# A two-block transformer kernel: 64 instead of 32 gathered tokens, 57 of 128 up tiles multiplied unsplit, and the second block's modulation read later

## The reference, cut to what matters

```python
q = (h2 @ w_query).reshape(T, 8, 2, 128)              # 256 tokens
sc = einsum('thpc,hpnc->thpn', q, sub_keys)           # scores against 2 x 128 keys
s1, i1 = top_k(sc[..., 0, :], 16); s2, i2 = top_k(sc[..., 1, :], 16)
cand = s1[..., :, None] + s2[..., None, :]            # 16 x 16 candidates per head
top_s, sel = top_k(cand, 16); idx = i1 * 128 + i2 of the selected
gates = softmax(top_s)
a = gelu(einsum('cd,chkd->chk', h2, expert_u[idx])) * gates
out = einsum('chk,chkd->cd', a, expert_v[idx])
x = x + gt2 * out
```

## Time and profile before

| | |
|---|---|
| median of three runs | 2063.39 us |
| profiled execution, its span | 2061.18 us, 2059.4 us |
| TensorE busy | 1984.0 us (96% of the span), 14228 matmul instructions |
| VectorE busy | 1667.9 us (81%) |
| ScalarE busy | 1270.3 us (62%) |
| GpSimd busy | 426.7 us (21%) |
| mean granted TensorE clock | 0.988 |
| moved by DMA | 476.51 MB, 231 GB/s in the mean |
| the chain that ended last | PE 75%, DVE 11%, ACT 5%, DMA 4%, issue 4%, POOL 2% |

### The profile page before, as it was taken

One profiled execution on the slowest core, in us unless ns is written; L12 is line 12 of the kernel. 1 busy time (PEld: TensorE's weight loads), 2 busy tenths in 40 slices (PEclk: granted clock), 3 DMA queues, 4 the chain that ended last, 5 costly groups with the idle time before them and its releaser, 6 DMA issues.

```text
span 2059.4 us, 37734 instructions
## 1 busy us (share of the span) xinstructions
PE 1984.0 (96%) x14228; PEld 1883.2 (91%) x14228; DVE 1667.9 (81%) x3456; ACT 1270.3 (62%) x2369; POOL 426.7 (21%) x384
## 2 busy tenths in 40 slices
PE   7999999999999999999989998999999999999997
PEld 5998999999999998999889898999999999999997
DVE  3777669898888888999779655699998898888886
ACT  3355556666999655555455454566669996555554
POOL 0000002425100133444100000034340001443340
PEclk9999999999999999999999999999999999999999
DMA  8765566666544699999766533666665446999994
GB/s 350 267 225 164 178 200 210 210 213 194 176 127 132 214 346 365 365 363 374 262 226 247 204 113 102 200 209 212 209 197 171 134 127 208 329 326 324 322 320 141
DMA packets 125156, 476.51 MB, mean 231 GB/s; under 512 B 13808, under 2 KB 14320, under 8 KB 120112
## 3 DMA queue, kind: packets, MB, share of 16 engines
q1 hardware_dynamic: 99168, 362.86, 52.8%
q0 software_dynamic: 20704, 80.55, 10.4%
q10 hardware_dynamic: 5104, 30.69, 3.9%
HBM read 472.14 MB, written 1.05 MB: 230 GB/s over the span
## 4 chain that ended last, share of the span: by engine, by line
PE 75%; DVE 11%; ACT 5%; DMA 4%; issue 4%; POOL 2%; ACTq 0%; DVEq 0%
PE PB L964 16%; PE PB L936 9%; PE PB L551 8%; PE PB L553 8%; PE PB L552 8%; PE PB L965 8%; PE PB L934 5%; PE PB L910 5%; DVE WL L1713 3%; DMA RING<-in_v 3%; ACT WH L1241 2%; PE PB L860 2%; POOL AR L2484 2%; PE PB L933 1%; DVE AR L1738 1%
## 5 line engine op out<-in xcount | busy, mean ns | idle before, releaser
L1713 DVE TENSOR_TENSOR WL<-RING,WH 128x1024 fp32r<-128x1024 f32 x651 | 801.7, 1232 | 262.1 <-ACT WH L1241 259.4
L1241 ACT ACTIVATE WH<-RING 128x1024 fp32r<-128x1024 f32 x651 | 686.8, 1056 | 390.3 <-PE PB L965 200.0
L964 PE MATMUL PB<-HX,WH 128*128 128x448 f32 x2048 | 646.8, 376 | 7.7 <-DVE WL L1713 6.5
L965 PE MATMUL PB<-HX,WL 128*128 128x224 f32 x2048 | 538.8, 263 | 0.0
L964 PEld LDWEIGHTS PB<-HX,WH 128*128 128x128 f32 x2048 | 383.7, 187 | 41.4 <-issue 11.0
L551 PE MATMUL PB<-HX,WH 128*128 128x224 f32 (+1 forms) x1360 | 394.7, 290 | 10.5 <-DVE HX L1792 5.7
L965 PEld LDWEIGHTS PB<-HX,WL 128*128 128x128 f32 x2048 | 390.2, 191 | 0.0
L552 PE MATMUL PB<-HX,WH 128*128 128x224 f32 (+1 forms) x1360 | 381.1, 280 | 0.0
L553 PE MATMUL PB<-HX,WL 128*128 128x224 f32 (+1 forms) x1360 | 381.0, 280 | 0.0
L936 PE MATMUL PB<-HX,WH 128*128 128x448 f32 x1162 | 375.6, 375 | 0.0
L934 PE MATMUL PB<-HX,WL 128*128 128x224 f32 x1328 | 326.3, 266 | 0.0
(11 more groups left out here) (265 smaller groups left out, 2712.7 us busy)
## 6 DMA issues: line engine op xcount, KB each, us to landing
RING<-in_u SPq DMA_DIRECT2D x256, 512.0 KB
RING<-in_v SPq DMA_DIRECT2D x256, 512.0 KB
RING<-in_win SPq DMA_DIRECT2D x90, 512.0 KB
AR<-in_wr ACTq DMA_DIRECT2D x24, 1024.0 KB, 7.9
RING<-in_wq SPq DMA_DIRECT2D x32, 512.0 KB
AR<-in_wr POOLq DMA_DIRECT2D x12, 1024.0 KB, 5.6
AR<-in_wm SPq DMA_DIRECT2D x8, 1024.0 KB, 16.3
RING<-in_wout SPq DMA_DIRECT2D x16, 512.0 KB
```

Source lines behind the costliest of these rows:

```text
L964: e.matmul(both_parts(c), hi(n_v + n)[:, cs], dense(k), start=start, stop=False)
L965: return e.matmul(PB[c][:, 0:T], lo(n_v + n)[:, cs], HH[:, k, 0:T], start=False, stop=stop)
L1241: e.activation(hi(t), raw(("w", t), words(t)), ACT.Copy).then_inc(s_hi, 1)
L1713: e.tensor_tensor(lo(t), raw(("w", t), words(t)), hi(t).bitcast(F32), ALU.subtract).then_inc(s_lo, 1)
```

## The change

`SP` becomes 64: 192 tokens are dense, 64 sparse; GK becomes 64, so 64 dots and 64 sums of gathered rows per block, and NQ becomes 48. Half 1 of the choice comes first, so the sparse tokens' experts are known after the first half of the choice. Then the indices are packed, brought to `SPX`, and the first three gathers issued, between the two halves on GpSimd. The dots stand beside the gates, at up tiles j = 83 to 127 (one or two in each); the 64 sums stay in the down stage, from tile 4 on. Up tiles with j >= 83 or j % 7 == 5 (45 and 12, together 57 in each block) are not split: TensorE waits for the tile in `RING` and multiplies it as fp32 with the unsplit activations `HT`. A ring slot that held such a tile is free when TensorE has used it. The modulation's chunks: 8 in the first block's down stage (from tile 12 on), 8 in the second mixer as before, and the last 8 beside the second mixer's gates, all eight in one buffer (`ar(0, 2, D)`), each issued when the one before is summed; `bcast(1, ...)` moves behind them, ahead of the output projection. Areas in `AR` move, `HT` and the choice's among them.

```diff
-SP = 32
+SP = 64
...
-SPARSE = {}
-for _m in range(N_GATHER):
-    SPARSE.setdefault(2 + _m * 119 // N_GATHER, []).append(_m)
-GELU_AT = 3 + GK * 119 // N_GATHER
+EARLY = 0
+DOT_AT = {}
+for _m in range(GK):
+    DOT_AT.setdefault(46 + 2 * _m if _m < EARLY else JG - 1 + (_m - EARLY) * (NK - JG + 1) // (GK - EARLY), []).append(_m)
+SUM_AT = {}
+for _m in range(GK, N_GATHER):
+    SUM_AT.setdefault(4 + (_m - GK) * 119 // GK, []).append(_m)
+GELU_AT = 2
+RAW = [j >= JG - 1 or j % 7 == 5 for j in range(NK)]
+RAW_TILE = [any(RAW[j] and n == w + j for w in (W_U, W2_U) for j in range(NK)) for n in range(N_TILES)]
...
-V_FIRST = 22
-N_IN_V = 12
+V_FIRST = 12
+N_IN_V = 8
+N_MID = 8
...
-WIDE = [j < JG - 1 for j in range(NK)]
+WIDE = [not RAW[j] for j in range(NK)]
...
# sync_program
-                    if was == "w":
-                        e.wait_ge(s_lo, n + 1)
+                    if was == "w" and RAW_TILE[n]:
+                        e.wait_ge(s_used, n + 1)
+                    elif was == "w":
+                        e.wait_ge(s_lo, SPLIT[n])
...
# tensor_program, peer
-                                r = three(PB[b][:, 0:T], wh[:, m, :], wl[:, m, :], HH[:, m, 0:T], HL[:, m, 0:T],
-                                          m == 0, m == KT - 1)
+                                r = e.matmul(PB[b][:, 0:T], w[:, m, :], HT[:, m, 0:T], start=m == 0, stop=m == KT - 1)
...
# tensor_program, second mixer: out of the Q tiles, to the output projection
-                if c == 0:
-                    bcast(1, (6, 7))
...
+            bcast(1, (0, 6))
...
# vector_program, choose: after the first half
+                    if o == 0:
+                        ts = slice(128 - SP, 128)
+                        own.done(own.n)
+                        e.wait_ge(s_gi, 2 * blk + 1)
+                        e.wait_ge(s_key, 4 * blk + 4)
...
# vector_program, peer: up tiles, after gates and times
+                    for m in DOT_AT.get(j, ()):
+                        gathered(m)
...
# vector_program, second mixer: late_sums() out at four of its 12 calls, one added after each pair of gate tiles
+                late_sums()
...
+            e.wait_ge(s_mdv, 24)
+            add_rows(48 + 2 * N_IN_V, 96, C_B2 + 2 * N_IN_V, 1)
+            e.wait_ge(s_mod, 10)
+            bcast(1, MC[:, 64:72])
...
# gpsimd_program, peer: between the halves, and at the end
+                    if o == 0:
+                        e.wait_ge(s_pk, blk + 1)
+                        for g in range(128 // SP):
+                            e.dma_start(SPX[SP * g:SP * g + SP, :, :], PK[128 - SP:128, g, :, :]).then_inc(s_sx, 16)
+                        e.wait_ge(s_sx, 16 * (128 // SP) * (blk + 1))
+                        gathers(N_BUF)
+                gathers(N_GATHER)
...
# gpsimd_program, between the blocks
+                if g < 24 + N_IN_V + N_MID:
+                    e.wait_ge(s_mdv, max(N_IN_V, g - 25))
+                else:
+                    e.wait_ge(s_mdv, g - 24)
+                    e.wait_ge(s_ps, 4)
```

More of the change, by code:

```diff
@@ L104 @@
 CHOICE = [80, 55] * 16 + [110, 150] + [105] * 8 + [55, 120] + [125, 125, 60, 125, 150, 125, 90] + [125, 125, 60, 125, 150, 125]
-CHOSEN = {len(CHOICE) * a + 43: a for a in range(2)}
+CHOSEN = {len(CHOICE) * o + 43: o for o in range(2)}
 def choice_turns():
@@ L1999, in choose @@
             def choose(blk):
-                for a in range(2):
+                for o in range(2):
+                    a = 1 - o
                     f2 = [0, 0]
@@ L2447, in peer, with gathers, beside @@
                     e.dma_start(HROW[SP * g:SP * g + SP, :], HROW[0:SP, :]).then_inc(s_hd, 16)
-                def add_halves(j0, j1):
+                issued = 0
+                def gathers(n):
+                    nonlocal issued
+                    for m in range(issued, n):
+                        M = N_GATHER * blk + m
+                        if M >= N_BUF:
+                            e.wait_ge(s_spent, M - N_BUF + 1)
+                        e.indirect_dma_start(
+                            out=GB[:, M % N_BUF, :], out_offset=None, in_=ur if m < GK else v,
+                            in_offset=bass.IndirectOffsetOnAxis(ap=SPX[:, 0, m % GK:m % GK + 1].bitcast(U32), axis=0),
+                        ).then_inc(s_gb[M % N_BUF], 16)
+                    issued = max(issued, n)
+                def beside(o, j0, j1):
                     for j in range(j0, j1):
@@ L2453, in add_halves @@
                             e.tensor_tensor(PG[:, j, :], PG[:, j, :], PG[:, j + 1, :], ALU.add).then_inc(s_sump, 1)
-                for a in range(2):
+                        if o:
+                            gathers(N_BUF + sum(len(DOT_AT.get(i, ())) for i in range(j + 1)))
+                for o in range(2):
+                    a = 1 - o
                     vv = V16[:, a, :, :].rearrange("p (h s) k -> p h s k", s=2)
                     ff = IF[:, a, :, :].rearrange("p (h s) k -> p h s k", s=2)
-                    if a == 0:
+                    if o == 0:
                         if blk:
```

156 lines of the change are left out of this document (74 added, 82 removed).

## The result

The changed kernel takes 2033.19 us (median of 4 runs, 2031.92 to 2035.52) against 2063.49 us (4 runs, 2061.83 to 2064.42) on the same chip: ratio 0.9855, 95% interval 0.9838 to 0.9872, 30 us less. The forecast was 2011 us. The direction was right, and a little more than half of the predicted gain of 52 us came: the time lies nearer to the 2038 us of the second rival than to the forecast.

A forecast was written before the change was run, and what follows sets the result against it. TensorE was taken to bound the feed-forward layers, VectorE close behind. Wide 2 x -16, narrow 2 x +14, down -29 and -25, mixer +4, GpSimd's pause +2 sum to -52: 2011 us, range 1960 to 2075.

The forecast's parts named there:

- the second rival: Both down stages give only half the forecast gain, VectorE waiting for ScalarE: -25 in all, 2038 us, chance 0.17.
- the prediction's sum: Wide up tiles per block: 159.8 us for 71 split tiles, 31.4 for 12 unsplit, 7.4 else: 198.6 us.
- Dense columns: Matmul pair of 384 and 192 columns: 0.281 us, between 0.275 and 0.2875, or 2.25 us per tile.
- Wide stage: Wide up tiles, per block: 198.6 us, a gain of 16, with GpSimd's pause costing 1 us.
- I put 1 us per block: GpSimd stops its additions about 10 us between the choice's halves; three banks cover some 4.5 us; cost 1 us (0 to 6).
- stays at 91%: VectorE in the wide up tiles: loses 12 splits of 1.23 us and keeps its busy share of 91%.
- Narrow stage: Up tiles with dots, per block: gathers' round of 9.5 us for three dots sets 195 us, 14 more than before.
- The first rival: All stages follow TensorE, gather rounds under 8.4 us: narrow up tiles 172 us, -109 in all, 1954 us, chance 0.15.
- Down stages: Down tiles: first block 307.5 us against 332, -25; second block -29, to 295 us.
- such a tile takes 2.48 us: First block's down tiles 12 to 76: 0.94 MB each at 378 GB/s, costing 15 us over TensorE's pace.
- Second mixer: Chunks before and beside the gates: -1 and +5 (0 to 25), together +4 us.
- The third: Rival: gathers' round of 12 us governs the narrow up tiles, 246 us each; +50 in all, 2113 us, chance 0.13.

The follow-up runs named there:

- e8_64_tokens: The kernel before with 64 sparse tokens instead of 32 and nothing else of the change: 2205.17 us, ratio 1.0684.
- e7_83_wide: The changed kernel with the 12 unsplit tiles of the wide stage split: 2039.86 us, ratio 0.9887 to the kernel before.

## Why the stages are as long as they are

**Wide stage: GpSimd's handover, and the clock.** GpSimd's timeline of the changed kernel, and of the experiment e1_spread in the same place (in brackets the idle time before, and what ended it):

```profile
399.60 1.13 POOL L2531 DMA_DIRECT2D SPX<-AR  x2 [5.88 <-DVE AR L2123]
405.49 1.01 POOL L2481 DMA_INDIRECT AR<-in_ur,SPX  x1 [4.76 <-DMA SPX<-AR]
...
408.07 0.94 POOL L2481 DMA_INDIRECT AR<-in_ur,SPX  x1 [0.30 <-issue]
409.04 0.59 POOL L2491 TENSOR_TENSOR AR<-AR 128x192 f32<-128x192 f32 x1
```

```profile
398.71 1.13 POOL L2533 DMA_DIRECT2D SPX<-AR  x2 [5.13 <-DVE AR L2123]
402.74 1.10 POOL L2491 TENSOR_TENSOR AR<-AR 128x192 f32<-128x192 f32 x1 [2.90 <-ACT AR L1264]
...
406.58 2.01 POOL L2481 DMA_INDIRECT AR<-in_ur,SPX  x1 [0.15 <-issue]
```

The windows of all engines from 396 to 412 and from 410 to 416 us, first the changed kernel, then e1_spread; then what ScalarE and TensorE wait for in the changed kernel:

```profile
396.00:412.00 16.00, 12.89 (x81) 12.45 (x80) 11.81 (x35) 7.92 (x14) 5.23 (x7) 0.92 0.76 266
410.00:416.00 6.00, 5.92 (x22) 5.92 (x23) 4.01 (x17) 3.59 (x8) 2.19 (x3) 0.50 0.86 321
```

```profile
396.00:412.00 16.00, 16.00 (x112) 16.00 (x111) 15.23 (x50) 9.84 (x20) 8.84 (x9) 1.00 0.76 254
410.00:416.00 6.00, 6.00 (x41) 6.00 (x40) 5.47 (x22) 4.09 (x7) 3.44 (x4) 1.00 0.90 309
```

```profile
409.66 0.36 ACT L1534 ACTIVATE AR<-AR 128x192 f32<-128x192 f32 x1 [5.40 <-POOL AR L2491]
410.08 0.69 PE L953 MATMUL PB<-HX,WH 128*128 128x384 f32 x1 [3.11 <-ACT AR L1534]
```

From 399.60 to 409.04 GpSimd is taken up with the indices and gathers, 9.4 us. In e1_spread its first addition comes at 402.74; here it comes at 409.04, 6.3 us later. ScalarE waits 5.40 us for it with its gelu, TensorE 3.11 us for a free bank: the banks cover half of the delay. When TensorE starts again, its granted clock is 0.50, the 1.2 GHz level, and it issues 22 matmuls in 6 us where e1_spread issues 41 at 1.00. By the tiles' starts, tiles 44 to 46 take 5.66, 4.44 and 3.14 us instead of 2.27 each: 6.4 us (6.5 in the second block), 3.4 of it in the tile that stands still and 3.0 in the two behind it at the lower clock. In a second profiled execution of the same kernel (c1_changed_again, below) the lower clock ends sooner in the first block, tiles 44 to 46 lose 4.4 us instead of 6.4, and the wide stage is 205.3 us instead of 208.0.

**Wide stage: VectorE where it chooses.** Without the pause, in e1_spread, the 83 tiles still take 205.5 us and not the 198.6 of the prediction's sum. Tiles 17, 30, 31, 70 to 72, 79 and 80 are long in the changed kernel and in e1_spread (2.5 to 3.8 us, where the wide ones around them take 2.3 to 2.4), and TensorE's waits in e1_spread's first wide stage are all for VectorE's splits: 4.8 us in 8 waits, against 1.7 in 3 before, when every tile but five (31, 37, 72, 79, 80) took 2.5 or 2.6 us. VectorE is busy for 178 of 207 us in the changed kernel's stage, 86% in the mean; these are the places where it is not in time. e8_64_tokens shows the same with all tiles split and no pause: its wide stages are 208.2 and 208.5 us, so columns that are cheaper by 20 us a stage gave 7.

**Narrow stage: the gathers' round.** The chain of waits from 503 to 701 us (start us, us, what), the totals of its first line, and the dots' line in both blocks:

```profile
by line: DMA AR<-in_ur,SPX 52.5%; issue 14.8%; DVE OH L2159 10.2%; DVE AR L2196 6.5%; PE PB L959 4.1%; POOL AR L2481 3.5%; DMA RING<-in_v 2.8%; DVE AR L2169 2.4%; DVE AR L2170 1.5%; DVE DOT L2196 1.0%; DVE AR L2177 0.8%; DVE WL L1732 0.6%; 
...
515.75 8.04 DMA AR<-in_ur,SPX
```

```profile
L2196 DVE CUSTOM_DVE_ANT_0 AR<-AR x64: 1203/1214/1227, 510.1 to 699.6; 128x1024 f32<-128x1024 f32 x64
```

```profile
L2196 DVE CUSTOM_DVE_ANT_0 AR<-AR x64: 1203/1222/1227, 1534.9 to 1717.5; 128x1024 f32<-128x1024 f32 x64
```

Half of the chain is gathers in flight, in pieces of 6 to 8 us. The 64 dots start 3.01 us apart in the first block (189.5 / 63), 2.90 in the second: rounds of 9.0 and 8.7 us, where 9.5 was predicted. In the waits VectorE stands 25.6 us (23 times) and 18.4 us (25 times) before a row that has not landed. In the first block these 25.6 us and its own 173.7 us of work fill the window of 198 us, so what the round adds is the waiting, and the work is 88% of the stage. The gathers' own landing, from the DMA issues of this window, is shorter than the 8.0 that the prediction used:

```profile
AR<-in_ur,SPX POOLq DMA_INDIRECT x61, 6.6
```

**Down stages: the chunks.** ScalarE's waits in the first and in the second down stage (line, waited for: us, times, longest), and four windows of the first:

```profile
ACT WH L1261 <- DMA RING<-in_v: 108.2, 74, 3.3
ACT WH L1261 <- PE PB L984: 23.5, 25, 3.3
```

```profile
ACT WH L1261 <- DMA RING<-in_v: 73.9, 57, 3.2
ACT WH L1261 <- PE PB L984: 47.0, 53, 1.5
```

```profile
726.00:746.00 20.00, 16.94 (x118) 16.52 (x116) 15.52 (x21) 10.68 (x15) 5.51 (x4) 1.00 1.01 391
746.00:786.00 40.00, 37.77 (x258) 36.52 (x257) 36.69 (x47) 20.61 (x33) 17.45 (x10) 1.00 0.99 376
826.00:866.00 40.00, 38.05 (x255) 36.28 (x254) 37.99 (x49) 20.88 (x33) 18.75 (x10) 1.00 0.99 377
894.00:994.00 100.00, 99.70 (x686) 99.08 (x685) 91.45 (x115) 55.70 (x86) 42.44 (x25) 1.00 0.97 346
```

By the tiles' starts, tiles 12 to 76 of the first stage take 2.57 us each, those of the second 2.28: 18 us of the 21 us between the two stages. The reader is to see two resources near their end: the DMA share is 0.99, and VectorE is busy 36.7 and 38.0 of 40 us. Behind the chunks VectorE is at 91.5 of 100 us at a pace of 2.33 us per tile (686 matmuls), 2.13 us of work per tile; a chunk every 8 tiles adds 2 x 1.22 / 8 = 0.31. That is 2.44 us, more than TensorE's 2.28, before a byte is counted. The prediction had only the bytes.

## The experiments

Ratios are to the kernel before, run beside each on the same chip.

**e1_spread.** GpSimd's wait and its three gathers are spread over the additions that follow:

```diff
-                        e.wait_ge(s_sx, 16 * (128 // SP) * (blk + 1))
-                        gathers(N_BUF)
 # in beside(), one gather per addition from tile 43 on
-                        if o:
-                            gathers(N_BUF + sum(...))
+                        if o and j > EQUALS[0][1] + 1:
+                            if not issued:
+                                e.wait_ge(s_sx, 16 * (128 // SP) * (blk + 1))
+                            gathers(min(j - EQUALS[0][1] - 1, N_BUF + sum(...)))
```

> GpSimd no longer stands still between the halves of the choice: it issues the two small DMAs of the indices at once, but waits for them and issues the first three gathers only later, one behind each of the additions for up tiles 43, 44 and 45. Theory (the pause stalls TensorE at tiles 43 to 46, where the trace of the changed kernel shows 13.2 us for three tiles instead of 6.8): both wide stages fall from 208 to about 202 us, the narrow and down stages stay; 2033 - 13 = 2020 us. Rival (the stall comes from VectorE's packing and the second half's start, not from GpSimd): both wide stages stay within 2 us of 208, 2031 us or more.

Measured: 2030.27 us (6 runs, 2014.62 to 2036.94), ratio 0.9825 [0.9795, 0.9855]. The stall is gone: both wide stages are 202.9 us, 5.1 and 5.2 less, and tiles 44 to 46 take 2.27 each. TensorE's clock stays at 1.00 there. So the pause, with the clock's fall behind it, is shown as the cause of 5 us per block, 2.4 and 4.9 if c1_changed_again is compared; 1 to 2 us of the 6.4 came back elsewhere, in tiles 50 to 53. For the whole the gain isn't clear of the scatter: 3 us against the changed kernel's first runs, 7 against its later ones (below), with overlapping intervals, not 10 to 13. In the profiled execution the down stages are 322.4 and 304.1, 3.3 and 6.1 longer. Part of that is the second pace of TensorE, told at the end.

**e4_two_buffers.** `N_BUF = 3` becomes 2.

> Two gather buffers instead of three. Theory (a dot in the narrow stage is paced by the buffers' round of about 8.9 us: landing 7.4, dot 1.2, reaction 0.3): a dot every 4.45 us, the narrow stages 197 and 191 become about 276 each; in the down stages a sum every 4.9 us instead of 4.6, some 10 us more each; 2033 + 165 + 20 = about 2215 us. Rival (VectorE's own 168 us of work sets the narrow stage and waits for gathers are slack): the narrow stages grow by less than 15 us, 2060 us at most.

Measured: 2162.99 us, ratio 1.0479 [1.0454, 1.0504]; narrow stages 231.7 and 224.2, down stages 350.3 and 337.7. The dots' line and the gathers' issue row of its first narrow stage:

```profile
L2196 DVE CUSTOM_DVE_ANT_0 AR<-AR x64: 1203/1224/1226, 507.0 to 730.5; 128x1024 f32<-128x1024 f32 x64
```

```profile
AR<-in_ur,SPX POOLq DMA_INDIRECT x62, 5.0
```

A dot comes every 3.55 us, a round of 7.1 for two buffers against 9.0 for three. One buffer less costs 34 us per narrow stage, so the round does set the pace. It costs less than the theory's 4.5 us per dot (276 us a stage), because a gather lands in 5.0 us when two are in flight and in 6.6 when three are: the landing is not a constant. Whether the other gathers or the whole traffic (246 against 287 GB/s) make the difference was not separated.

**e6_spread_early.** As e1_spread, and the first 8 dots stand at up tiles 52, 54, ..., 66.

```diff
-EARLY = 0
+EARLY = 8
-    DOT_AT.setdefault(46 + 2 * _m if _m < EARLY else ...
+    DOT_AT.setdefault(52 + 2 * _m if _m < EARLY else ...
```

> As e1_spread, and the first 8 of the 64 dots stand in the wide stage, at up tiles 52, 54, ... 66, so that 56 are left for the narrow one. Theory (the buffers' round paces the narrow stage): eight dots fewer at 2.97 us are 24 us, until VectorE's 158 us and TensorE's 161 us of own work bind at about 172: narrow 175 and 172 us; the wide stages pay 10 us of VectorE at 91% busy, 0 to 6 us each; with the 13 us of e1: about 1992 us. Rival (VectorE's sum over the whole up stage binds): what the narrow stages lose the wide ones gain, 2018 us.

Measured: 2005.01 us (5 runs, 2001.46 to 2006.59), ratio 0.9708 [0.9691, 0.9725]. Its windows of the first wide and both narrow stages:

```profile
295.00:505.00 210.00, 198.97 (x1345) 194.87 (x1344) 189.00 (x538) 124.63 (x226) 96.43 (x104) 1.00 0.71 237
505.00:684.00 179.00, 168.00 (x1133) 165.32 (x1133) 158.87 (x452) 107.58 (x334) 61.79 (x56) 0.99 0.85 296
...
1514.00:1691.00 177.00, 166.59 (x1127) 164.21 (x1125) 157.87 (x450) 107.11 (x334) 60.10 (x56) 0.99 0.85 297
```

Against e1_spread the narrow stages lose 19.1 and 14.6 us (178.1, 177.2), about 2.1 us per dot moved, and the wide ones gain 7.5 and 8.8 (210.4, 211.7), about 1 us per dot. Together 17 us; the whole is 25 us faster on the same chip, since the down stages came out 7 us shorter too. That is halfway between theory (1992) and rival (2018): the narrow stages stop at 178 and 177 and not 175 and 172, and the wide ones pay more than 0 to 6 us. The round held the narrow stage, as the 2.1 us per dot against VectorE's own 1.2 show. Beside the wide tiles VectorE spends the dot's own time and waits for no gather.

**e5_small_chunks.** The eight chunks of the first down stage (24 to 31) bring 128 of 1024 columns, so the second block's modulation lacks the rest; their sums still run over 1024.

```diff
             def rows_in(g, done=0):
...
+                if g >= 24:
+                    e.dma_start(row_chunk(g)[:, :, 0:128], row_source(g)[:, :, 0:128]).then_inc(...)
+                    return
```

> The eight chunks of the second block's modulation in the first down stage are loaded with an eighth of their columns (the other columns of the area are not loaded, so the second block's modulation is not the reference's); their VectorE sums stay. Theory (bytes: the first down stage runs at 365 to 370 GB/s and a DMA share of 0.98 while the chunks come): the first down stage falls from 319 to about 301 us, near the second's 298; 2015 us. Rival (the chunks' 16 VectorE sums, 19 us of it, make the difference): the stage stays above 315 us, 2030 us.

Measured: 2022.73 us, ratio 0.9812 [0.9787, 0.9837]. **e10_half_v** takes bytes from the same stage in another way, from the gathers for the sums (the indices are not doubled, so it also brings other rows than the ones wanted, as many and half as long):

```diff
-                            out=GB[:, M % N_BUF, :], out_offset=None, in_=ur if m < GK else v,
+                            out=GB[:, M % N_BUF, 0:D // 2 if m >= GK else D], out_offset=None,
+                            in_=(ur if m < GK else v).rearrange("n (t d) -> (n t) d", t=2) if m >= GK else (ur if m < GK else v),
```

> The changed kernel, but the 64 gathers of rows for the sums bring 512 of 1024 columns (as many gathers, 0.26 MB each instead of 0.52; the sums still run over 1024 columns, so the sparse tokens' second half isn't computed). 16.8 MB less in each down stage. Theory (the first down stage is bound by the bytes: DMA share 0.96 to 1.01 at 359 to 391 GB/s from tile 12 to 76, where a tile takes 2.57 us instead of 2.28): these 64 tiles go back to 2.30, first down stage 319 to 302, second 298 to 295, 2013 in all (2008 to 2018). Rival (the time goes to ScalarE and VectorE, which have the chunks' staging and sums there: 8 x (copies + 2 x 1.22 us)): first down stage over 312 us, 2028.

Measured: 2015.21 us (4 runs, 2009.18 to 2026.47), ratio 0.9754 [0.9726, 0.9782]. The first down stage of both profiled executions, e5_small_chunks first, then e10_half_v with ScalarE's waits in it:

```profile
691.00:1003.00 312.00, 301.50 (x2068) 296.31 (x2069) 278.69 (x360) 171.71 (x264) 135.68 (x64) 0.99 0.92 336
```

```profile
697.00:1009.00 312.00, 299.25 (x2071) 294.34 (x2072) 279.06 (x360) 172.30 (x264) 134.14 (x64) 1.00 0.87 307
```

```profile
ACT WH L1261 <- DMA RING<-in_v: 50.2, 34, 4.1
```

By the tiles' starts the first down stage is 311.7 and 311.5 us, 7.5 less than 319.1 in both (5.4 less than the 317.0 of c1_changed_again), and not the 301 or 302 of the theory. With 7 to 9 MB less in tiles 12 to 76, these tiles still take 2.45 us in e5_small_chunks and 2.51 in e10_half_v, where the DMA share is 0.87 and the ring's waits are halved (108.2 to 50.2): 7 and 4 us less of their 18. The rest of e10_half_v's gain lies mostly behind the chunks, at TensorE's faster pace (told at the end). So bytes account for 4 to 7 us of the 18. The rest follows VectorE's load of 2.44 us per tile, which is what e5_small_chunks runs at, or the chunks' own landings. A part of it is VectorE's by the tiles' starts: tiles 17, 37, 45, 61 and 69 take 2.7 to 2.8 us in the changed kernel and in both experiments, bytes or no bytes, and each stands right behind a chunk's second sum. How the rest divides was not separated.

**e12_chunks_wider** asks it by spacing (built on e11_every_third, below):

```diff
-IN_V = {V_FIRST + 8 * i + 4 * (i > 0): 24 + i for i in range(N_IN_V)}
+IN_V = {V_FIRST + 12 * i + 4 * (i > 0): 24 + i for i in range(N_IN_V)}
```

> As e11_every_third, but the 8 chunks of the first down stage are fetched and summed one in 12 tiles (to tile 100) instead of one in 8 (to tile 76). Theory (bytes bound it there: 0.94 MB per tile now over 64 tiles at 2.57 us, which is 367 GB/s; one chunk in 12 tiles is 0.89 MB, 2.43 us over 96 tiles against TensorE's 2.28): 14.4 us of loss instead of 18.2, 4 us less than e11_every_third. Rival (each chunk costs a fixed 2 us by its staging and sums, however far apart): the same as e11_every_third within 1.5 us.

Measured: 2007.09 us (5 runs, 2001.20 to 2010.79), ratio 0.9717 [0.9699, 0.9735] against 0.9699 [0.9673, 0.9725] for e11_every_third: no gain, and the first down stage is 322.3 us against 319.9. The rival holds: eight chunks cost some 2.3 us each (18 us over 64 tiles), spread or not, and long tiles behind the second sums move along (17, 45, 69 and 93 take 2.8 us here). That is close to the 2.44 us that VectorE spends on one; it is not shown that this is all of why.

**e9_narrow_split.** The 45 tiles from j = 83 on are split again:

```diff
+                                if j >= JG - 1:
+                                    r = three(PB[b][:, 0:T], wh[:, m, :], wl[:, m, :], HH[:, m, 0:T], HL[:, m, 0:T],
+                                              m == 0, m == KT - 1)
+                                    continue
                                 r = e.matmul(PB[b][:, 0:T], w[:, m, :], HT[:, m, 0:T], start=m == 0, stop=m == KT - 1)
```

> The changed kernel, but the 45 up tiles from j = 83 on are split again (three products of the split parts of 192 columns instead of one fp32 product), the 12 earlier ones stay unsplit. TensorE's own work stays: 45 x 24 x 0.11 = 119 us against 118. VectorE gets 43 splits of 1.23 us: 168 + 53 = 221 us. Theory (VectorE then is the bound of the narrow stage): 225 to 232 us against 197.4 and 190.7, +64 over both blocks: 2097 (2085 to 2110). Rival (the gathers' round is the bound and its waits of 25.6 and 18.4 us on VectorE take the splits in; unsplit tiles bought only the rest): 205 to 210 us, 2058 at most.

Measured: 2088.72 us, ratio 1.0120 [1.0092, 1.0147]; narrow stages 221.2 and 219.5 us. The first one's window and VectorE's two costliest groups in it (us, mean ns, idle before):

```profile
500.00:721.00 221.00, 186.60 (x1489) 182.26 (x1487) 217.05 (x511) 148.48 (x378) 91.95 (x63) 0.94 0.75 262
```

```profile
L2200 DVE CUSTOM_DVE_ANT_0 AR<-AR 128x1024 f32<-128x1024 f32 x64 | 77.1, 1222 | 2.4 <-DMA AR<-in_ur,SPX 2.3
L1736 DVE TENSOR_TENSOR WL<-RING,WH 128x1024 fp32r<-128x1024 f32 x47 | 57.5, 1224 | 1.5 <-ACT WH L1265 1.4
```

VectorE is busy 217 of 221 us and the wait for gathers fell from 25.6 to 2.3: it is the bound, as the theory has it; the splits cost 52 us over both blocks and not 64, since those waits took some of them in. Unsplit tiles are worth 52 us here, on VectorE and not on TensorE.

**e7_83_wide.** The 12 unsplit tiles of the wide stage are split: `RAW = [j >= JG - 1 for j in range(NK)]`.

> The changed kernel, but all 83 up tiles ahead of the narrow stage are split and wide (none of them is an fp32 product). An fp32 tile takes TensorE 2.60 us from start to start, a wide one 2.27: 12 x 0.33 = 4 us per block less on TensorE. VectorE gets 12 splits of 1.23 us back: 178.7 + 14.8 = 193.5 us of a stage of 208.2. Theory: VectorE has the room, since its idle time in this stage is 29 us and only four or five places hold TensorE up; the wide stage goes to 204 to 208 us and the whole to 2029 (2025 to 2034): the 12 unsplit tiles of the change bought nothing. Rival: VectorE's splits are late at the places of the choice and every split put back is a stall, +12 to +15 us per block: 2060.

Measured: 2039.86 us (4 runs, 2036.90 to 2047.65), ratio 0.9887 [0.9854, 0.9921]; the window of its first wide stage:

```profile
296.00:507.00 211.00, 202.74 (x1360) 194.90 (x1359) 194.02 (x540) 140.21 (x251) 93.32 (x102) 1.00 0.71 219
```

211.4 and 210.8 us. Over the same 83 tiles the changed kernel takes 210.6 and 210.7, and 207.9 and 210.5 in c1_changed_again. So the stage stays above the theory's 204 to 208, but its conclusion holds more nearly than the rival's (220 or more): with the pause in place those 12 tiles are worth at most 1 us a block against the one profile and 3.5 in one block against the other, within what two executions of one kernel differ by, and the ratios' intervals overlap (0.9887 here, 0.9855 and 0.9859 there). VectorE at 92% is late now and then: TensorE waits 5.2 us for its splits instead of 3.6.

**e8_64_tokens.** The kernel before with `SP = 64` alone. `DOT` and `GEL` lie in `PK`, `ROWS2` lies elsewhere, and four waits count one activation step more, for room.

> The kernel before with 64 sparse tokens instead of 32 and nothing else of the change: all tiles split, the sparse half chosen last, the 64 dots and 64 sums of gathered rows all in the down stage. Theory (the gathers' round of three buffers sets a pace of 3.16 us per row): 128 rows x 3.16 = 405 us for a down stage that was 332 and 324.5, +77 per block; the wide stage 215 to 203 and the narrow one 181 to 173 with 192 dense columns, -20 per block: 2063 + 2 x 57 = 2177 (2150 to 2200). Rival (VectorE's time is the bound, not the round): its 289 us in the down stage + 64 x 1.22 = 367, +38 per block: 2099.

Measured: 2205.17 us, ratio 1.0684 [1.0648, 1.0719]. Its two narrow-stage and down-stage windows, first block:

```profile
503.00:670.00 167.00, 165.82 (x1470) 164.73 (x1469) 146.38 (x385) 146.59 (x377) 4.41 (x5) 1.00 0.47 157
670.00:1113.00 443.00, 343.81 (x2066) 326.11 (x2067) 363.09 (x503) 173.11 (x265) 242.97 (x127) 0.92 0.92 334
```

The wide stages get 7 us shorter, the narrow ones 14, and the down stages grow by 111 and 73, to 443.5 and 397.4: 3.46 and 3.10 us per gathered row, VectorE busy 363 of 443. The round sets the pace there too, and the theory's 405 was too low for the first block, where chunks come on top. So more sparse tokens alone cost 142 us. What makes the change a gain is that the dots found another stage, which the earlier choice and the unsplit tiles' free VectorE allow.

**e11_every_third** (early dots at 47, 50, ..., 68) and **e14_early12** (12 of them, at 46, 48, ..., 68), with **c1_changed_again**, the changed kernel itself, on one chip. Each is one line's change of e6_spread_early's:

```diff
-    DOT_AT.setdefault(52 + 2 * _m if _m < EARLY else ...
+    DOT_AT.setdefault(47 + 3 * _m if _m < EARLY else ...
```

> As e6_spread_early, but the 8 early dots stand at up tiles 47, 50, ..., 68 instead of 52, 54, ..., 66. There every tile with a dot took 3.1 to 4.1 us and the next 2.4 to 2.6 instead of 2.27, 7.5 us per block over e1_spread. Theory (VectorE is over its time only where a dot comes every second tile: 178 of 203 us is 88%, a dot of 1.21 us per 4.5 us adds 27%; one per 6.8 us adds 18%): half of the 7.5 us goes, wide stage 206 to 207, narrow stage 178 as there, 1998 in all (1994 to 2003). Rival (a dot costs its time wherever it stands, or the first row hasn't landed at tile 47): no change or worse, 2005 or above.

> As e11_every_third, but 12 early dots, at up tiles 46, 48, ..., 68. Theory (the narrow stage is at its floor once the gathers' round is covered: with 56 dots it took 178 us, of which TensorE's own work is 161 and VectorE's 159): 52 dots leave it at 174 to 177, the wide stage takes 4 x 1.2 us more and VectorE's crowding returns, 213: 2006 (2002 to 2012), above e11_every_third. Rival (each early dot still takes 2.4 us from the narrow stage, as the first 8 did, for 0.9 us in the wide one): 1992.

> The changed kernel itself, on the chip that runs the other three. Theory: 2033 us (2031 to 2036). By this the gain of the experiments is read on one chip; were it at 2025 or 2040, the differences of 10 us that were read across chips wouldn't stand.

Measured: e11_every_third 2003.09 us (6 runs, 1992.84 to 2011.62), ratio 0.9699 [0.9673, 0.9725]; e14_early12 2000.28 (4 runs, 1992.63 to 2009.36), 0.9670 [0.9649, 0.9691]; the changed kernel 2037.08 (5 runs, 2026.23 to 2041.02), 0.9859 [0.9838, 0.9879], the same ratio as at first. The changed kernel came out 1 us above the 2031 to 2036 expected of it, so differences of a few us between chips are read by the ratios alone. Wide stages 209.9 and 208.2 for every third, 217.8 and 215.6 for twelve; the narrow ones 174.7 and 177.7, and 170.9 and 168.4.

Eight dots at every third tile cost the wide stages 7.0 and 5.3 us, at every second 7.5 and 8.8: crowding is a small part, and the theory (206 to 207 us) fell in both blocks. From 8 to 12 dots the narrow stages give 4 and 9 us, below the floor of 174 that the theory of e14_early12 named, and the wide ones take 8 and 7. The intervals of all three early versions meet: 2000 to 2005 us is one result, some 1.6% under the changed kernel and 3% under the one before.

## Why the prediction was right, and where it was off

The direction, the price of the unsplit tiles and the gathers' round were right. The size was not: the time fell by 30 us and not 52, and the sum of the rivals' second (-25, 2038 us) came nearer to it. Two terms were too good, wide and first down stage, and what was better than forecast in the second narrow stage and the mixer hid a third of that.

- **Dense columns.** 0.281 us was 0.285: the small matmul gains nothing below 224 columns. 2.28 instead of 2.25 is 4 us per down stage.
- **Wide stage.** The largest miss, 10 us in each block. Two steps failed. One is "I put 1 us per block" on GpSimd's pause (0 to 6): it is 6.4 and 6.5, and e1_spread takes 5.1 back. The pause was sized rightly at 10 us (9.4 measured), and the first addition due came some 3 us into it, a tile or two later as said; the banks covered 3 us and not 4.5, and the lower clock behind TensorE's stop, 3.0 of the 6.4 us, was not in the sum at all. The other is that VectorE "stays at 91%", taken as no loss: its mean share is 86%, but at the places of the choice its splits are late, which is most of the other 5 us (4.8 us of waits, and slower tiles behind them; e8_64_tokens has it without a pause). The tiles between these places are right (2.27 and 2.6).
- **Narrow stage.** Right: 195.0 against 195 in the first block, 188.2 in the second, with VectorE waiting for gathers. The round is 9.0 and 8.7 against 9.5, because from a gather's issue to the next dot in its buffer it is some 7.4 us and not 8.0. That the first block came out to the microsecond is luck: 63 steps of 3.01 us are less than the 193 us counted, and 4 us before the first dot and 1 to 2 behind the last make it up. e4_two_buffers and e6_spread_early show the mechanism from both sides. The first rival, that all follows TensorE, is out by these.
- **Down stages.** The second: 298.0 against 295, the difference being the pair. The first: 319.1 against 307.5. The mis-sized term is "such a tile takes 2.48 us": it takes 2.57, 5.5 us over the 64 tiles; the tiles up to 120 behind them, at 2.34 instead of 2.25 and mostly at TensorE's slower pace, make 4 more. The step took the fullest stretch's 378 GB/s as the only limit; VectorE's sums ask 2.44 us of such a tile as well, and e5_small_chunks and e10_half_v show 2.45 and 2.51 with bytes gone. As for the rule of the Trainium skill that was weighed there ("DMA: Bandwidth & Descriptors", Specifications: 358 GB/s of HBM per core): 0.94 MB at that rate is 2.63 us by its figure, a first down stage 9 us longer than mine, an estimate from that page, so it came nearer to the length; but the windows show 376, 377 and 391 GB/s, so the trace does not agree with it as a limit. By the note in the same page's section "Measured" the figure is the share of a core whose neighbour is streaming too, and one alone gets more, which fits this kernel on one core.
- **Second mixer.** +0.3 instead of +4: the late chunks' landing beside the gates is 5.2 us in the median (5.6 in the earlier trace rows), and the seven microseconds of lag were covered.
- The second rival (down stages give half) was right for the first block alone, and its 2038 us came near by the wide stages' loss, which is none of its own. The third, slower by the gathers' round, would have needed a round of 10.8; e8_64_tokens is what that looks like, with 3 x 3.46 = 10.4 us.

## What to carry to other kernels

A chain "buffer free, issue, landing, use" has a pace of its own, round over number of buffers; work out that pace before work is moved next to it, and move the first few uses ahead to where nobody waits. Where an in-order engine serves a pipeline with little slack (three banks here), count a wait put into its program from the first thing due to the one that comes late, take the slack off, and add what the clock costs if TensorE comes to stand: here 3.4 us of standing and 3.0 us at half the clock. A mean busy share of 86% does not say that an engine has room where the work is dense; make the sum place by place. Where an extra job is priced by its bytes, price its time on the busiest engine of that stage too, and take the greater.

## What the runs showed of the hardware

**TensorE has two paces at one granted clock.** The changed kernel and e10_half_v from 1800 to 1900 us, both without idle time on TensorE and with a clock of 1.00:

```profile
1800.00:1900.00 100.00, 100.00 (x705) 100.00 (x704) 90.76 (x112) 56.55 (x87) 45.60 (x24) 1.00 0.97 354
```

```profile
1800.00:1900.00 100.00, 100.00 (x691) 100.00 (x691) 89.94 (x110) 56.71 (x87) 45.16 (x23) 1.00 0.86 289
```

The same pairs come every 0.284 us in one and every 0.289 in the other. The pace can hold for a whole stage, and it changes between tiles of 2.27 and 2.31 or 2.32 us within one execution, nearly always where TensorE was held up: of 34 such changes in the down stages of the changed kernel and its experiments, 33 have a tile of over 2.35 us between the two paces. With the slower one the second down stage of e10_half_v is 300.7 us although it has fewer waits than the 298.0 of the changed kernel. What selects the one or the other at such a tile isn't known from these runs. In the kernel before, with 448 and 224 columns, a tile takes 2.51 us in the second down stage throughout.

**A stop of TensorE is followed by half the clock.** In the changed kernel TensorE stands for 3.11 us before 410.08, and then works from 410 to 416 us at a granted clock of 0.50, the 1.2 GHz level, with 22 matmuls where 41 would go; the same happens in the second block (tile 44 takes 6.19 us, and the clock is 0.50 from 1435 to 1440). In e1_spread, where TensorE isn't stopped at this place, the clock stays at 1.00. Waits of up to 1.2 us on splits, as e1_spread has in its wide stages, were not followed by it.

**The changed kernels scatter more.** Runs of the kernel before lie between 2059.7 and 2070.5 us (29 runs beside the experiments), the changed kernel between 2026 and 2041, e1_spread between 2015 and 2037. More of their time hangs on landings, and the two paces come on top.

**What a gather holds of GpSimd differs.** Its instructions that issue the gathers of `ur` take 1.10 us in the mean (128 of them, most 0.94), those of `v` 1.90 (1.98 in the earlier trace rows), for the same bytes and packets. It goes with the stage and not with the table: in the kernel before and in e8_64_tokens, where the gathers of `ur` stand in the down stage, most take 1.98 and 1.95 us, and in e9_narrow_split, where VectorE is busy 217 of 221 us of the narrow stage, most take 1.68. Why is open.
